# Fifteen words of padding in place of eight: moving every SBUF tensor behind the parameters

## The reference

```python
def first_block(x, c, ctx, ...):          # two layers
    for l in range(2):
        h  = modulate(rmsnorm(x, g1), sh1, sc1)
        z  = h @ w_in                      # nine groups of 256 columns
        mix = concat(mixer_a(z), mixer_b(z), mixer_c(z), differential_attention(z))
        x  = x + gt1 * (mix @ w_out)
        x  = x + gt2 * conv_ffn(modulate(rmsnorm(x, g2), sh2, sc2))   # 1024 -> 2*2816 -> 1024
    return rmsnorm(x, final_g)

def second_block(x, c, ctx, ...):         # one layer
    x = x + g1 * (mLSTM and window attention, gated, merged, @ w_out)
    h = modulate(rmsnorm(x), sh2, sc2)
    # _peer: 8 heads pick 16 of 16384 experts for each token
    act = gelu(h @ peer_u.T); w = g * act; x = x + g2 * (w @ peer_v)
```

## The kernel before

| tensor | bytes | starts at | modulo 512 |
|---|---|---|---|
| RAW | 16384 | 16512 | 128 |
| TH | 12288 | 32896 | 128 |
| TL | 12288 | 45184 | 128 |
| PAD0 | 448 | 57472 | 128 |
| HXh | 8192 | 57920 | 64 |
| P | 3684 | 82496 | 64 |
| ADA0 | 384 | 86208 | 192 |
| SM | 352 | 87232 | 192 |
| PAD1 | 32 | 87584 | 32 |
| AROW0 | 512 | 87616 | 64 |
| X, G | 16384, 131072 | 88640 | 64 |
| Hh | 16384 | 105024 | 64 |
| l0midh, l1midh | 16384 | 159808 | 64 |
| mqa | 4096 | 206272 | 448 |
| W | 6144 | 219712 | 64 |

## Time and profile before

### The profile page before, as it was taken

The page is one execution under the profiler, slowest core; times in us unless marked ns, Lnnn a source line. Parts: engine busy times, 40 slices in busy tenths (PEclk is TensorE's granted clock), DMA queues, the critical chain, the costliest instruction groups (busy, mean ns, idle before and its releaser), DMA issues.

```text
span 2184.2 us, 42595 instructions
## 1 busy us (share of the span) xinstructions
PE 2094.0 (96%) x18040; PEld 1987.5 (91%) x18040; DVE 1436.1 (66%) x2728; ACT 1085.3 (50%) x1879; POOL 480.6 (22%) x226
## 2 busy tenths in 40 slices
PE   7999999999998989999889988999999999999998
PEld 5977999999998789999778888999999999999998
DVE  3445478877785666666663656589388897666665
ACT  5333352232335455546433445555577776555564
POOL 1201100000011120001211341188766662000000
PEclk9999999999998999999999999999999999999999
DMA  7245345566663345654221234555444445555553
GB/s 275 104 139 180 117 164 185 172 223 227 207 222 118 115 145 205 225 196 134 83 70 58 78 109 161 175 193 190 168 140 146 150 146 174 194 193 194 194 194 134
DMA packets 97278, 354.90 MB, mean 162 GB/s; under 512 B 10688, under 2 KB 11712, under 8 KB 96704
## 3 DMA queue, kind: packets, MB, share of 16 engines
q1 hardware_dynamic: 97088, 352.18, 47.9%
HBM read 351.09 MB, written 1.05 MB: 161 GB/s over the span
## 4 chain that ended last, share of the span: by engine, by line
PE 86%; DVE 5%; ACT 3%; issue 3%; DMA 2%; POOL 2%; SPq 0%; ACTq 0%; DVEq 0%; POOLq 0%
PE ps L79 82%; PE ps L84 3%; DVE TL L113 1%; PE ps L106 1%; ACT TH L157 1%; POOL TL L113 1%; DMA RAW<-in_wada 1%; ACT SQ L154 1%; DMA AW<-in_wada 1%; POOL SM L113 0%; ACT Hh L157 0%; DMA RAW<-in_wdn 0%; DVE ps L113 0%; DMA RAW<-in_wup 0%; DVE SQ L113 0%
## 5 line engine op out<-in xcount | busy, mean ns | idle before, releaser
L157 ACT ACTIVATE TH<-RAW 128x1024 fp32r<-128x1024 f32 (+1 forms) x515 | 539.8, 1049 | 281.8 <-PE ps L79 253.6
L113 DVE TENSOR_TENSOR TL<-RAW,TH 128x1024 fp32r<-128x1024 f32 (+1 forms) x343 | 424.5, 1238 | 238.1 <-ACT TH L157 237.2
L113 POOL TENSOR_TENSOR TL<-RAW,TH 128x1024 fp32r<-128x1024 f32 x172 | 413.2, 2405 | 507.2 <-ACT TH L157 481.2
L79 PE MATMUL ps<-Hh,TL 128*128 128x256 f32 x1920 | 450.3, 287 | 17.2 <-DVE TL L113 8.5
L79 PE MATMUL ps<-Hl,TH 128*128 128x256 f32 x1920 | 439.5, 281 | 0.0
L79 PE MATMUL ps<-Hh,TH 128*128 128x256 f32 x1920 | 439.4, 281 | 0.0
L79 PE MATMUL ps<-HXh,TL 128*128 128x256 f32 x1314 | 365.6, 282 | 7.0 <-POOL TL L113 3.1
L79 PEld LDWEIGHTS ps<-Hh,TL 128*128 128x128 f32 x1920 | 322.7, 192 | 42.9 <-issue 17.9
L79 PE MATMUL ps<-HXh,TH 128*128 128x256 f32 x1314 | 360.0, 278 | 0.0
L79 PE MATMUL ps<-HXl,TH 128*128 128x256 f32 x1314 | 359.9, 278 | 0.0
L79 PE MATMUL ps<-W,TH 128*128 128x256 f32 x2052 | 349.1, 276 | 0.0
(11 more groups left out here) (335 smaller groups left out, 3112.4 us busy)
## 6 DMA issues: line engine op xcount, KB each, us to landing
RAW<-in_ut SPq DMA_DIRECT2D x128, 512.0 KB, 3.3
RAW<-in_v SPq DMA_DIRECT2D x128, 512.0 KB, 3.3
RAW<-in_wup SPq DMA_DIRECT2D x88, 512.0 KB, 4.3
AV<-in_wada SPq DMA_DIRECT2D x80, 512.0 KB, 3.8
RAW<-in_win SPq DMA_DIRECT2D x74, 512.0 KB, 3.5
RAW<-in_wada SPq DMA_DIRECT2D x56, 512.0 KB, 3.6
RAW<-in_wdn SPq DMA_DIRECT2D x32, 512.0 KB, 4.4
RAW<-in_wout SPq DMA_DIRECT2D x24, 512.0 KB, 3.7
```

What stands on the lines that cost most here:

```text
L79: return self.e.matmul(out, lhs, rhs, start=first, stop=last, skip_group_check=skip)
L113: return DRY if self.e is None else self.e.tensor_tensor(out, a, b, op)
L157: return DRY if self.e is None else self.e.activation(out, a, ACT.Copy, **kw)
```

## The change

Seven more words are asked for in the unused tensor `PAD1`; no instruction is added, removed or reordered. The words of the change name its aim as a start at 64 modulo 512 bytes.

```diff
     MOD = sb("MOD", 64)
     SM = sb("SM", 88)
-    sb("PAD1", 8)
+    sb("PAD1", 15)
     AROW = [sb(f"AROW{i}", 128) for i in range(2)]
```

## The result

The changed kernel takes 2220.9 us in the median of four runs (2219.64 to 2225.53), the kernel before 2183.82 in its four (2179.78 to 2190.16): a ratio of 1.0171, 95% interval 1.0142 to 1.0200. The profiled execution took 2219.64 us with a span of 2217.9. Each engine's instructions and their order are the same. In the program, X starts at byte 88672, Hh at 105056, W at 219744, all 96 modulo 512; HXh, TH and TL stay at 57920, 32896 and 45184. So the tensors moved by 32 bytes as foretold.

The account below looks back on a forecast made before the run. TensorE, busy 2094.0 of 2184.2 us, was taken to bound the kernel. Matmuls 0, VectorE and ScalarE 0 and DMA 0 left the forecast at 2186 us, with an 8 in 10 range of 2171 to 2212.

Parts of the forecast that it names:

- What bounds the kernel: Whole kernel: TensorE, busy 2094.0 of 2184.2 us and carrying 86% of the chain.
- Where the memory goes: SBUF layout: room rounds to 32 bytes, so tensors behind PAD1 move by 32, from 64 to 96 modulo 512.
- Matmuls that stream moved rows: Hh, Hl, mid, mixer, nMG and W matmuls, 10,806 together: cost taken as 0, bounds -14.7 to +33 us.
- The row that I took it from: Trace pair of rows starting at 448 and 64, both 378 ns in the median; taken to show the start doesn't matter.
- isn't a matter of address: Wide split matmuls: the same tiles, HXh against TH, take 281 ns in one stretch and 276 in the next.
- The upper bound: Moved matmuls: all go at the slower pace, 7,480 added at 4.4 to 4.5 ns, +33 us.
- The first rival: Feed-forward and expert stages: moved rows make more restarts lock into 117.8 ns, up to 2218 us; chance 0.28.
- the sign asked for: Profile after: a new third start distance besides 113.3 and 117.8, or W at 281 ns, would show slow moved rows.
- VectorE and ScalarE: Their work on moved tensors: 0; at 2 ns on some 4,600 instructions, less than 1 us of path.
- DMAs: Transfers into moved tensors AV, AW, X, C and context: 0, at most 2 us of path.
- the 0.2 that I held to be the price of the offset: AV transfers: bound of 0.2 us a tile up or down, 80 x 0.2 = 16 us of transfer, hidden.
- The 16-byte lines: SBUF access: a penalty per 16-byte line crossed; 64 and 96 are both multiples of 16, so nothing changes.

Follow-up runs that it names:

- The scan: Layouts of the kernel before, varying the bytes from the start of weights TH, TL to the start of the rows, modulo 512: medians 2183.8 to 2243.3 us.
- 0: Kernel before with PAD1 at 24 words, all rows behind it at 128 modulo 512 like the weights: 2243.33 us, ratio 1.0270.
- +128: Kernel before with PAD1 at 56 words, rows behind it at 256 modulo 512, weights at 128: 2232.53 us, ratio 1.0205.
- -96: Kernel before with PAD1 left out, rows behind it at 32 modulo 512, weights at 128: 2223.89 us, ratio 1.0159.
- +32: Kernel before with PAD1 at 32 words, rows behind it at 160 modulo 512, weights at 128: 2212.78 us, ratio 1.0106.
- +192: Kernel before with PAD1 at 72 words, rows behind it at 320 modulo 512, weights at 128: 2187.80 us, ratio 0.9992.
- +64: Kernel before with PAD1 at 40 words, rows behind it at 192 modulo 512, weights at 128: 2204.33 us, ratio 1.0076.
- -192: Kernel before with PAD0 at 80 words, HX and all rows at 448 modulo 512, weights at 128: 2211.89 us, ratio 1.0093.
- -48: Kernel before with TH and TL cut 16 bytes later, at 144 modulo 512, HX and all rows at 96: 2239.42 us, ratio 1.0233.
- -80: Kernel before with TH and TL cut 16 bytes later, at 144 modulo 512, all rows kept at 64: 2243.02 us, ratio 1.0255.

## Why the prediction was wrong, point by point

**What bounds the kernel**: right. TensorE bound it, and its 36.2 us of added busy time are the loss.

**Where the memory goes**: right. The room is rounded, the tensors went from 64 to 96, and the stated aim was met by the kernel before and undone by the change.

**Matmuls that stream moved rows, the step that failed: "I take 0".** Measured, 37.0 us of added excess (from 15.2 to 52.2) for 10,806 matmuls, 3.4 ns each. The row that I took it from does not speak of this case. The mqa and l1q rows differ by 384 bytes in the place of the rows, but both stream past C, at 64: their distances are -128 and 0. The scan shows 0 to be bad for split matmuls, and +128 too (-128 isn't in it), so the row compares two places of which neither need be clear. It is also of 8 and 4 lone matmuls of another kind, read by their length, where the loss is in how closely one follows another. Beside it the text held that the pace "isn't a matter of address", because both paces occur at the same addresses. That is true for the choice between 113.3 and 117.8 at distance -64; it doesn't follow that another distance leaves this choice in place, and it didn't.

**The upper bound**, +33 us, was short: it let all moved matmuls go at 117.8, the slowest that the trace showed. They go at 118.33, and 10,800 times the further 0.5 ns are 5 us. The range ended at 2212, below even this bound, and the time fell 9 us outside.

**The first rival**, "the moved rows go slowly", with 0.28, has the outcome: its place (W, which had held 113.3 nearly throughout), its sign, and its 2218 against 2220.9. Its mechanism, more restarts that lock into 117.8, is not what happened; it is a new distance between starts that no restart escapes. That it has to do with the weight loads was named there, and the runs bear that out; and the sign asked for, a new third distance between starts, is there. The close 2218 is in part luck: the pace behind it, 117.8, was the old one. The price of 120.0 at distance 0 shows that 118.33 was not its end.

**VectorE and ScalarE**: right. X<-ps,ADA,X keeps its median of 483 ns, and the shifted taps stay at 484; the line of X before, then both after:

```profile
L125 DVE SCALAR_TENSOR_TENSOR X<-ps,ADA,X x104: 467/483/488, 224.8 to 1343.1; 128x256 f32<-128x256 f32 x104
...
L125 DVE SCALAR_TENSOR_TENSOR l1cv<-XX,P,l1cv x4: 484/484/2534, 771.0 to 780.3; 128x255 f32<-128x255 f32 x4
...
L125 DVE SCALAR_TENSOR_TENSOR X<-ps,ADA,X x104: 469/483/488, 229.2 to 1362.8; 128x256 f32<-128x256 f32 x104
```

**DMAs**: right in the sum. AV lands in 3.8 us as before:

```profile
AV<-in_wada SPq DMA_DIRECT2D x80, 512.0 KB, 3.8
...
RAW<-in_wada SPq DMA_DIRECT2D x56, 512.0 KB, 3.8
```

RAW, which didn't move, went from 3.6 to 3.8 for the same tiles, so the 0.2 that I held to be the price of the offset comes without any offset; that it is a matter of when the tiles are asked for is a guess. The rule of the Trainium skill's "DMA: Bandwidth & Descriptors", section "How a descriptor splits into AXI transactions", asked for under 1%; no run here resolves that. Nor did it make the 0.2 us between AV and RAW before the change: by that rule a row of 4096 bytes that starts at 64 costs fewer beats than one that starts at 128, yet AV, at 64, was the slower, 3.8 us against RAW's 3.6.

**The 16-byte lines** of the Trainium skill's "SBUF — State Buffer", section "SBUF: two separate sides", were cited for no change. At 64 and 96, both multiples of 16, the time differs by 1.7%, so that rule is not the one that bears on this. The same page of the Trainium skill, in the table of "A bandwidth-pool intuition that's wrong (but worth ruling out)", gives weight loads a second, independent read port. Whoever takes from it that the two reads can't slow each other is not borne out: with rows and weights read side by side, W's matmuls take between 113.3 and 120.0 ns by the addresses alone. The measurement decides that; whether it is the port or the memory behind it, no run here tells.

**Shown and not shown.** Shown: the loss of the change sits in the matmuls whose rows were moved, and follows the distance between the rows and TH and TL, not the place of either (moved together by 32 bytes they cost nothing). Argued only: that the two reads meet in the same part of the memory. Open: why -96 and +32, or 0 and +128, differ though they are 128 bytes apart; whether weights that start at 16 modulo 32 are slow at any distance; and what decides how many restarts take the slower of the two paces at distances of 64 modulo 128 (excess 18 to 48 us). No layout tried beats the kernel before.

## What to carry to other kernels

Where matmuls follow one another without a gap, each with its own weight load, check where the streamed rows start relative to the weights; here 64 modulo 128 bytes apart gave W the quick pace, at no cost for -64 and +192 but 0.8% for +64 and 0.9% for -192 through the other rows, and every other distance tried cost 1 to 2.7%. Read the addresses from the program and don't add up sizes by hand: rounding to 32 bytes made a correct layout look wrong. And a row of the trace bounds a cost only if it varies what the change varies: here the pair had different starts, but what mattered was the difference of starts from the weights, and the pair had -128 and 0 where the change went from -64 to -32.

## What the runs showed of the hardware that was not expected

- In W's stage the distance between starts of 128x256 matmuls with a weight load each, at a granted clock of 1.00, depends on the byte distance of the two operands: 120.0 ns at 0, 118.3 at -32, 118.3 at -48 and 118.7 at -80 (both with weights at 144), 117.8 at -96, 116.7 at +32, 118.7 at +128, and 113.3 at -64, +64, +192 and -192.
- At the last four there are two steady paces, 113.3 and 117.8, and a stall can change one for the other. Only the W stage takes the quick one almost always. At -48 the other rows have two as well, about 118 and 123.4.
- Moving the weights by 16 bytes cost 2.6%, moving both weights and rows by 32 nothing measurable (1.0008, 0.9991 to 1.0025).
